# Two more expert blocks loaded ahead of the last load of the first mixer, and sums of squares made as columns

## The chip, the core and the metric

The kernel runs on one core of a Trainium2 chip. Its time is device microseconds (us) of one execution. Before the change three runs took 1422.38, 1422.58 and 1422.58 us; the median is 1422.58 us. One further execution was recorded by the hardware profiler; every row below comes from it.

## What is computed

Two transformer blocks on one sequence of 256 tokens with 1024 channels, all in float32. Only the parts that the change touches are shown.

```
# block 1
u = modulate(rmsnorm(h, g_norm1), sh1, sc1)
y = hybrid_mixer(u, ...)            # ends with:  merged = gate0*y_conv + gate1*y_gla ;  y = merged @ w_out
h = h + ga1 * y
u2 = modulate(rmsnorm(h, g_norm2), sh2, sc2)
h = h + ga2 * hierarchical_moe(u2)  # 4 groups x 8 experts, top 2 inside the best group
x = modulate(rmsnorm(h, g_final), shf, scf)
# block 2
x = x + mixer2(rmsnorm_2(x, ln1_g)) ;  x = x + conv_ffn(rmsnorm_2(x, ln2_g)) ;  return rmsnorm_2(x, final_g)

rmsnorm(x, g) = x * rsqrt(mean(x*x) + 1e-6) * g
# routing: lg = u2 @ w_rg + b_rg ;  le = u2 @ w_re + b_re   (4 + 32 columns)
# experts: hid = silu(t @ w1[e]) * (t @ w3[e]) ;  y += comb[:, e] * (hid @ w2[e])
#          w1, w3: 32 x 1024 x 512, w2: 32 x 512 x 1024 (float32), all of them are read
```

## The kernel before

**Layout.** Activations lie turned: 128 channels on the partitions, 8 tiles of them, 256 tokens along the row (`h`, `u`, `sq`). The whole memory of a partition is one tensor `arena` of 40870 columns, cut by hand, and a pair of regions that follow each other in time at its end (`fine1`, then `above`; then `fine2`). Most projections split each weight piece into a high part (ScalarE) and a rest (VectorE) and make three products for each pair; `advance(name, n)` on an engine does its share for n pieces, `flush` finishes what is begun. A piece is 8 x 256 columns (1 MiB). Pieces arrive in a ring of three slots of 2048 columns (`ring`, at the start of `arena`).

**The experts.** Their 192 MiB come as 96 blocks of 2 MiB (`WIDE` = 4096 columns), 12 for each of 8 quads of experts: four of w1, four of w3, four of w2. `wides` holds 8 places; block n goes to place n mod 8. Block n of 8 and more waits until TensorE is done with block n - 8 (`up_made`, `down_made`). The first three blocks have places that come free early (`early`) and are issued among the loads of the first mixer; place 3 is columns 0 to 4095, that is two slots of the ring, free when the last piece of `w_out` is split; places 4 to 6 are `above`, free when the last products of `w_out` are made (`products_of[PIECES1 - 1, 1]`); place 7 waits for a sum of the norm.

**The loads.** Every load of weights is issued by SyncE in one fixed order (`sync_program`); a load that waits holds back all loads behind it. `ada(j)` loads the two half chunks 2j and 2j + 1 of the modulation weights (1 MiB each); chunks 24 to 31 (`w_ada_f`) are loaded between the pieces `pw`, `gla_o` and `w_out` and summed by TensorE in `ada_sums(12)` to `ada_sums(15)`, each of which frees a slot for a later chunk.

**The norms.** `norm(i)` on TensorE multiplies a 128 x 128 matrix of ones with the squares (8 products of 256 columns), which gives the sum over channels on all partitions; ScalarE takes the root of 128 x 256, VectorE the reciprocal of 128 x 256 (`rstd`) and multiplies. Norm 0 opens block 1; norm 1 is ahead of the routing and is spelled out by itself; norms 2 and 3 stand between the experts and block 2; norm 4 is ahead of the convolutional FFN. `spin(n)` issues n products that nobody reads. After norm 1 the logits are made as 36 rows of 256 tokens, scaled by `rstd`, given a bias, and turned by TensorE to columns (tokens on the partitions); `rstd` itself is also turned.

## Time and profile before

| | us |
|---|---|
| median of three runs | 1422.58 |
| profiled execution, its time | 1423.39 |
| its span | 1421.6 |
| TensorE busy (matmuls) | 1207.6 (85%) |
| VectorE busy | 675.5 (48%) |
| ScalarE busy | 449.9 (32%) |
| the chain that ended last: TensorE, DMA, VectorE, SyncE's queue | 56%, 18%, 12%, 7% of the span |

In the rows, PE is TensorE's matmuls and PEld its weight loads, DVE is VectorE, ACT is ScalarE, SPq is SyncE's issuing of DMAs. A line such as L1293 or L2098 is that of a helper through which an engine's operations pass, so operations are told apart by shape and time. A float32 matmul stands in the trace as two records, a float32r one and a transpose as one. PEclk is the share of full clock granted to TensorE.

### The profile page before, as it was taken

Reading aid. Unit: us, or ns where it says so; the run is one execution under the profiler, and the core shown is the slowest. Engines: PE = TensorE matmul, PEld = TensorE weight load, DVE = VectorE, ACT = ScalarE, POOL = GpSimd, SP = SyncE. Lnnn points to the kernel's source line nnn. Section 1 sums busy time; section 2 is a strip of 40 time slices with the busy share of each in tenths; the row PEclk is TensorE's granted clock in tenths of the full one; section 3 lists DMA queues with packets and bytes.
Section 4 is the critical chain, followed back from the end, with each engine's and each line's share of the span. In section 5 each row is a group of like instructions: output and inputs, shape, how many; then the busy total and the mean of one; then the engine's idle time right before and its main releaser. Section 6 shows DMA issues by size and latency. Waiting matters only on the chain.

```text
span 1421.6 us, 20416 instructions
## 1 busy us (share of the span) xinstructions
PE 1207.6 (85%) x8784; PEld 955.0 (67%) x8784; DVE 675.5 (48%) x1146; ACT 449.9 (32%) x643; POOL 2.2 (0%) x16
## 2 busy tenths in 40 slices
PE   6999999999765657566575899999999999999998
PEld 3789897886322213222231599899998889999986
DVE  2657986554110101101010464465657786668974
ACT  2543343432000000000000353443545454555453
POOL 0000000000000000000000000000000000000000
PEclk9999999999988878788897999999999999999999
DMA  9887862978999999999999676343543425355552
GB/s 350 302 284 264 269 149 106 360 246 356 420 420 420 419 420 420 420 420 420 419 420 416 221 223 191 111 129 119 162 155 114 149 94 196 115 174 179 183 204 87
DMA packets 169555, 374.06 MB, mean 263 GB/s; under 512 B 8257, under 2 KB 121299, under 8 KB 145780
## 3 DMA queue, kind: packets, MB, share of 16 engines
q1 hardware_dynamic: 166940, 369.12, 70.4%
q0 software_dynamic: 144, 3.54, 0.8%
q8 instruction: 71, 1.16, 0.4%
q10 hardware_dynamic: 2376, 0.04, 0.1%
q14 instruction: 24, 0.20, 0.0%
HBM read 371.59 MB, written 4.62 MB: 265 GB/s over the span
## 4 chain that ended last, share of the span: by engine, by line
PE 56%; DMA 18%; DVE 12%; SPq 7%; ACT 4%; issue 2%; DVEq 0%; ACTq 0%
PE bank L617 30%; DMA arena<-in_w 13%; SPq L2638 7%; PE bank L1270 4%; DVE arena L1301 4%; PE bank L930 4%; DVE fine L1293 3%; ACT fine L2098 2%; DVE arena L1293 2%; DMA above<-in_w 2%; PE bank L971 2%; PE bank L614 2%; PE bank L897 2%; DVE arena L1298 1%; PE bank L648 1%
## 5 line engine op out<-in xcount | busy, mean ns | idle before, releaser
L617 PE MATMUL bank<-fine 128*128 128x256 f32 x4512 | 561.5, 286 | 17.4 <-DVE fine L1293 17.4
L617 PEld LDWEIGHTS bank<-fine 128*128 128x128 f32 x4512 | 550.6, 194 | 31.1 <-issue 21.6
L1293 DVE TENSOR_TENSOR fine<-arena,fine 128x1024 fp32r<-128x1024 f32 (+2 forms) x263 | 299.7, 1168 | 175.2 <-ACT fine L2098 165.8
L2098 ACT ACTIVATE fine<-arena 128x1024 fp32r<-128x1024 f32 (+2 forms) x279 | 266.5, 984 | 183.8 <-PE bank L617 84.6
L2098 ACT ACTIVATE arena<-bank 128x256 f32<-128x256 f32 (+2 forms) x153 | 68.0, 472 | 530.0 <-PE bank L942 187.4
L930 PE MATMUL bank<-arena 128*32 128x512 f32 x640 | 123.4, 795 | 56.8 <-DMA arena<-in_w 37.5
L1293 DVE TENSOR_TENSOR arena<-arena,bank 128x512 f32<-128x512 f32 x8 | 8.4, 1053 | 288.8 <-PE bank L930 288.8
L930 PE MATMUL bank<-above,arena 128*32 128x512 f32 x384 | 77.1, 734 | 56.8 <-issue 24.7
L2098 ACT ACTIVATE arena<-arena 128x512 f32<-128x512 f32 (+6 forms) x90 | 61.1, 708 | 152.0 <-DVE arena L1301 63.1
L1301 DVE SCALAR_TENSOR_TENSOR arena<-arena 128x256 f32<-128x256 f32 (+3 forms) x262 | 107.6, 484 | 1.1 <-ACT arena L2098 0.8
L930 PEld LDWEIGHTS bank<-arena 128*32 128x32 f32 x640 | 30.6, 140 | 112.8 <-issue 111.5
L930 PEld LDWEIGHTS bank<-above,arena 128*32 128x32 f32 x384 | 20.1, 131 | 111.2 <-issue 109.1
L1293 DVE TENSOR_TENSOR arena<-arena 128x512 f32<-128x512 f32 (+7 forms) x130 | 82.6, 661 | 9.3 <-ACT arena L2098 7.9
L1293 DVE TENSOR_TENSOR arena<-bank,arena 128x256 f32<-128x256 f32 (+8 forms) x92 | 36.8, 436 | 49.5 <-PE bank L1078 17.6
L1270 PE MATMUL bank<-fine 128*128 128x512 f32 x264 | 60.3, 390 | 0.0
L971 PE MATMUL bank<-arena 128*32 128x512 f32 x304 | 46.6, 667 | 14.3 <-DMA arena<-in_w 10.9
L1779 DVE COPY arena<-bank 128x512 f32<-128x512 f32 x8 | 5.5, 692 | 107.6 <-PE bank L971 92.3
L1270 PEld LDWEIGHTS bank<-fine 128*128 128x128 f32 x264 | 49.4, 188 | 10.7 <-DVE fine L1293 0.3
L614 PE MATMUL bank<-fine 128*128 128x256 f32 x384 | 47.6, 284 | 1.0 <-DVE fine L1293 1.0
L614 PEld LDWEIGHTS bank<-fine 128*128 128x128 f32 x384 | 46.5, 192 | 2.0 <-issue 2.0
L565 PE MATMUL bank<-arena 128*128 128x256 f32 x152 | 38.3, 393 | 0.8 <-ACT arena L2098 0.8
L1298 DVE TENSOR_SCALAR arena<-bank,arena 128x128 f32<-128x128 f32 x96 | 30.9, 385 | 16.9 <-PE bank L897 16.6
(177 smaller groups left out, 810.8 us busy)
## 6 DMA issues: line engine op xcount, KB each, us to landing
arena<-in_w SPq DMA_DIRECT2D x118, 1024.0 KB, 26.5
above<-in_w SPq DMA_DIRECT2D x66, 1024.0 KB, 26.5
arena<-in_w_in SPq DMA_DIRECT2D x62, 1024.0 KB, 5.5
arena<-in_w_ada SPq DMA_DIRECT2D x24, 1024.0 KB, 9.6
arena<-in_ffn_w_up SPq DMA_DIRECT2D x22, 1024.0 KB, 5.1
arena<-in_ffn_w_down SPq DMA_DIRECT2D x11, 1024.0 KB, 5.0
arena<-in_w_ada_f SPq DMA_DIRECT2D x8, 1024.0 KB, 9.4
above<-in_w SPq DMA_DIRECT2D x12, 512.0 KB, 17.9
```

Source lines behind the costliest of these rows:

```text
L565: e.matmul(bank[:, 0:256], ident, consts[:, 0:256], start=True, stop=True, skip_group_check=True)
L614: ins = e.matmul(o, x[:, kt, j * P:j * P + P], w[:, k, :], start=start, stop=stop, skip_group_check=True)
L617: ins = e.matmul(o, w[:, k, j * P:j * P + P], x[:, kt, :], start=start, stop=stop, skip_group_check=True)
L897: ins = e.matmul(bank[:, j * P:j * P + P], uT[:, tc, k * P:k * P + P], hot2[:, tc, quad * P:quad * P + P], start=tc == 0, stop=tc == 1)
L930: ins = e.matmul(bank[32 * x:32 * x + 32, :], xg[:, i, 4 * th + k, 32 * x:32 * x + 32], slots[x // 2][:, x % 2, k, :], start=th == 0 and k ...
L971: ins = e.matmul(ob[c][32 * x:32 * x + 32, :], hidT[:, i, 2 * th + k, 32 * x:32 * x + 32], slots[x // 2][:, x % 2, k, 512 * c:512 * c + 51 ...
L1270: ins = e.matmul(obs[tc][c][:, :], x, w[:, cs], start=n == i == 0, stop=n == 21 and i == 2, skip_group_check=True)
L1293: return e.tensor_tensor(o, a, b, f)
L1298: return e.tensor_scalar(o, a, s_1, s_2, f1, f2)
L1301: return e.scalar_tensor_tensor(out=o, in0=a, scalar=s, in1=b, op0=f1, op1=f2)
L2098: return e.activation(o, i, f, bias=bias, scale=scale)
L2638: e.dma_start(slot[:, x, :, :], src[quad, :, 2 * (i % 2) + x, at:at + kt, :]).then_inc(*wide_in[s].up(n, 16))
```

## The change

The places of the blocks and the loads: `early` gets a fourth place, where `q`, `kk` and `v` of the first mixer lay, and the fifth block goes to slots 1 and 2 of the ring, free once the last piece but one of `w_out` is split. The place that waited for a sum of the norm is gone. Of the two half chunks behind `ada(12)` the second comes behind the loads of `pw`; the first three blocks of `w_out` come ahead of the third expert block. The norms: the squares become the stationary operand and one column of ones the moving one, so that a norm's sum is two columns with tokens on the partitions; root and reciprocal are of 128 x 2, and `as_row` brings the result back as a 128 x 256 row tile in PSUM, from which VectorE multiplies. The routing keeps columns throughout. Three warm-up groups of six products: one stays, two become two.

```diff
-        ada_slots2 = [arena[:, q_at:q_at + SLOT], flat(v), arena[:, consts1_at:consts1_at + SLOT]]
+        ada_slots2 = [arena[:, xbase:xbase + SLOT], arena[:, consts1_at:consts1_at + SLOT], flat(u)]
...
-        early = [arena[:, at:at + WIDE] for at in (early_at + WIDE, early_at + 2 * WIDE, early_at)]
-        wides = early + [arena[:, 0:WIDE]] + [above[:, WIDE * i:WIDE * i + WIDE] for i in range(FINE // WIDE)] + [
-            arena[:, WIDE:2 * WIDE]]
+        early = [arena[:, at:at + WIDE] for at in (early_at + WIDE, early_at + 2 * WIDE, early_at, q_at)]
+        wides = early + [arena[:, SLOT:SLOT + WIDE]] + [above[:, WIDE * i:WIDE * i + WIDE] for i in range(FINE // WIDE)]
...
-                    ins = e.matmul(bank[:, 0:256], ones, squares[:, k, :], start=k == 0, stop=k == KT - 1)
+                    for tc in range(2):
+                        ins = e.matmul(bank[:, tc:tc + 1], squares[:, k, tc * P:tc * P + P], ones[:, 0:1], start=k == tc == 0,
+                                       stop=k == KT - 1, skip_group_check=True)
...
+            def as_row(o, tc):
+
+                return e.matmul(o, rstd_of[:, tc:tc + 1].to_broadcast([P, P]), ident, start=True, stop=True, skip_group_check=True)
...
-                    ins = e.matmul(raw[0:36, 0:256], wr[:, k, :], h[:, k, :], start=k == 0, stop=k == KT - 1)
+                    for tc in range(2):
+                        ins = e.matmul(raw[:, 36 * tc:36 * tc + 36], h[:, k, tc * P:tc * P + P], wr[:, k, :], start=k == tc == 0,
+                                       stop=k == KT - 1, skip_group_check=True)
...
             norm(2)
+            norm_row(2)
             spin(6)
             norm(3, u)
-            spin(6)
+            norm_row(3)
+            spin(2)
...
             norm(4)
-            spin(6)
+            norm_row(4)
+            spin(2)
...
-                e.reciprocal(rstd, rstd).then_inc(*normed.up((i, "r")))
-                e.wait_ge(*normed[i, "r"])
+                e.reciprocal(rstd_of, rstd_of).then_inc(*normed.up((i, "r")))
+                e.wait_ge(*rms_row[i])
                 for g in range(2):
-                    tt(sq[:, 4 * g:4 * g + 4, :], x[:, 4 * g:4 * g + 4, :], repeat(rstd, 4), ALU.mult).then_inc(*normed.up((i, g)))
+                    tt(sq[:, 4 * g:4 * g + 4, :], repeat(bank_of(normed, (i, 1))[:, 0:256], 4), x[:, 4 * g:4 * g + 4, :],
+                       ALU.mult).then_inc(*normed.up((i, g)))
...
+                    elif f == 25:
+                        e.wait_ge(*act_on["conv"])
                     elif f == 26:
-                        e.wait_ge(*act_on["conv"])
+                        e.wait_ge(*x_lo_v["og", 1])
...
-            ada(12)
+            ada(12, (0,))
             load("pw", 2)
+            ada(12, (1,))
...
-            load("gla_o", 1)
+            load("gla_o", 2)
+            ada(14)
+            load("w_out", 3)
+            ada(15)
+            load("w_out", 1)
             expert(0, 2)
-            load("gla_o", 1)
-            ada(14)
-            load("w_out", 2)
-            ada(15)
-            load("w_out", 2)
+            expert(0, 3)
```

**The loads on SyncE, from `pw` to the end of the first mixer.** `in_w` is an expert block (two DMAs each), `in_w_ada_f` a half chunk. Before:

```order
L2600 DMA arena<-in_w_gla_o 128x8x256 [waits conv_out]
L2638 DMA arena<-in_w 128x2048 [waits o_turned]
L2638 DMA arena<-in_w 128x2048
L2600 DMA arena<-in_w_gla_o 128x8x256 [waits w_lo_by_vector]
L2581 DMA arena<-in_w_ada_f 128x4x512 [waits ada_sum] x2
L2600 DMA arena<-in_w_out 128x8x256 [waits w_lo_by_vector] x2
L2581 DMA arena<-in_w_ada_f 128x4x512 [waits ada_sum] x2
L2600 DMA arena<-in_w_out 128x8x256 [waits w_lo_by_vector] x2
L2638 DMA arena<-in_w 128x2048 [waits w_lo_by_vector]
L2638 DMA arena<-in_w 128x2048
L2638 DMA above<-in_w 128x2048 [waits products]
```

The same place now:

```order
L2632 DMA arena<-in_w_gla_o 128x8x256 [waits conv_out]
L2632 DMA arena<-in_w_gla_o 128x8x256 [waits w_lo_by_vector]
L2613 DMA arena<-in_w_ada_f 128x4x512 [waits ada_sum] x2
L2632 DMA arena<-in_w_out 128x8x256 [waits w_lo_by_vector] x3
L2613 DMA arena<-in_w_ada_f 128x4x512 [waits ada_sum] x2
L2632 DMA arena<-in_w_out 128x8x256 [waits w_lo_by_vector]
L2670 DMA arena<-in_w 128x2048 [waits o_turned]
L2670 DMA arena<-in_w 128x2048
L2670 DMA arena<-in_w 128x2048 [waits o_turned]
L2670 DMA arena<-in_w 128x2048
L2670 DMA arena<-in_w 128x2048 [waits w_lo_by_vector]
```

The third block went behind `w_out`, the fourth joins it there, and the fifth waits for VectorE instead of standing behind the last split piece.

**TensorE from the raw logits to the ranks of the routing.** Before:

```order
L851 MATMUL bank<-arena 36x256 x4
L858 MATMUL bank<-arena 128x256
L860 MATMUL bank<-arena 128x256
L851 MATMUL bank<-arena 36x256 x4
L867 MATMUL bank<-arena 128x128 x8
L875 MATMUL bank<-arena 128x1 x2
L880 MATMUL bank<-arena 128x36 x2
L867 MATMUL bank<-arena 128x128 x8
L565 MATMUL bank<-arena 128x256 x4
L888 MATMUL bank<-arena 128x64
```

Now (L873 are the raw logits, L879 the squares, L896 the turning of `h`):

```order
L873 MATMUL bank<-arena 128x36 x8
L879 MATMUL bank<-arena 128x1 x4
L873 MATMUL bank<-arena 128x36 x8
L896 MATMUL bank<-arena 128x128 x16
L567 MATMUL bank<-arena 128x256 x4
L907 MATMUL bank<-arena 128x64
```

The two turnings (L875, L880) between the halves of the turning of `h` are gone, and the sums have twice the products.

## Rows read from the trace of the kernel before

**Rows 1.** The page: GB/s of DMA in 40 slices of 35.5 us.
```profile
GB/s 350 302 284 264 269 149 106 360 246 356 420 420 420 419 420 420 420 420 420 419 420 416 221 223 191 111 129 119 162 155 114 149 94 196 115 174 179 183 204 87
```
**Rows 2.** Stretches: length, busy time per engine (count), PEclk, DMA share, GB/s.
```profile
309.00:321.00 12.00, 12.00 (x103) 12.00 (x102) 6.12 (x9) 4.70 (x6) 0.00 (x0) 1.00 0.01 2
...
329.00:330.00 1.00, 1.00 (x6) 0.52 (x5) 0.96 (x4) 0.49 (x1) 0.00 (x0) 1.00 0.71 106
330.00:331.00 1.00, 1.00 (x5) 0.58 (x4) 0.67 (x2) 0.98 (x2) 0.00 (x0) 1.00 0.78 221
331.00:332.00 1.00, 1.00 (x6) 0.44 (x5) 0.00 (x0) 0.92 (x2) 0.00 (x0) 1.00 0.92 385
```
**Rows 3.** Timeline of SyncE's queue: start, length, line, DMAs issued.
```profile
328.59 3.21 SPq L2638 DMA_DIRECT2D above<-in_w  x6
...
346.63 8.64 SPq L2638 DMA_DIRECT2D arena<-in_w  x8
```
**Rows 4.** Timeline of TensorE, 268 to 331 us: start, length, [idle before, releaser].
```profile
275.24 1.07 PE L648 MATMUL bank<-arena 128*32 128x512 f32 x8 [0.42 <-DMA arena<-in_w_ada_f]
276.24 20.42 PE L617 MATMUL bank<-fine 128*128 128x256 f32 x168
296.58 1.92 PE L648 MATMUL bank<-arena 128*32 128x512 f32 x16
301.80 4.56 PE L617 MATMUL bank<-fine 128*128 128x256 f32 x24 [3.29 <-DVE fine L1293]
...
308.14 20.42 PE L617 MATMUL bank<-fine 128*128 128x256 f32 x168
```
**Rows 5.** A stretch inside the 4.56 us of rows 4.
```profile
303.00:304.50 1.50, 1.50 (x9) 1.50 (x9) 0.40 (x1) 1.48 (x2) 0.00 (x0) 0.50 1.10 356
```
**Rows 6.** Source line L2600 (loads of pieces), 236 to 330 us.
```profile
DMA to landing us min/median/max: 5.2/11.0/15.4
```
**Rows 7.** Timeline of ScalarE, 236 to 330 us.
```profile
247.99 3.97 ACT L2098 ACTIVATE arena<-arena 128x256 f32<-128x256 f32 x6 [1.78 <-DVE arena L1293]
...
295.73 2.95 ACT L2098 ACTIVATE fine<-arena 128x1024 fp32r<-128x1024 f32 x3 [6.43 <-DMA arena<-in_w_out]
```
**Rows 8.** Timeline of all engines, 319 to 354 us (routing, first expert products).
```profile
331.40 1.92 PE L851 MATMUL bank<-arena 128*36 128x256 f32 x8
...
334.19 0.51 PE L875 MATMUL bank<-arena 128*128 128x1 f32 x4
...
335.49 0.17 DVE L1689 TENSOR_REDUCE arena<-bank 128x2 f32<-128x8 f32 x1 [0.79 <-PE bank L880]
...
336.75 1.89 PE L565 MATMUL bank<-arena 128*128 128x256 f32 x8
...
338.79 0.43 PE L888 MATMUL bank<-arena 128*128 128x64 f32 x2
...
342.94 3.65 PE L930 MATMUL bank<-arena 128*32 128x512 f32 x32 [0.30 <-DVE arena L1298]
```
**Rows 9.** Timeline of all engines, 764 to 826 us (norms 2 and 3).
```profile
806.70 2.00 ACT L2098 ACTIVATE fine<-arena 128x1024 fp32r<-128x1024 f32 x2 [2.21 <-DMA arena<-in_w_in]
...
813.86 0.47 ACT L2098 ACTIVATE arena<-bank,arena 128x256 f32<-128x256 f32 x1 [1.22 <-PE bank L669]
...
816.23 2.36 DVE L1293 TENSOR_TENSOR arena<-arena 128x1024 f32<-128x1024 f32 x2
```
**Rows 10.** Groups by form, whole program: total busy, mean ns, idle before.
```profile
L1740 DVE RECIPROCAL arena<-arena 128x2 f32<-128x2 f32 x1 | 0.2, 167 | 0.0
...
L1293 DVE TENSOR_TENSOR arena<-bank,arena 128x512 f32<-128x512 f32 x16 | 10.7, 689 | 21.8 <-PE bank L1078 7.3 <-PE bank L1270 6.6 <-PE bank L1165 5.5
...
L1293 DVE TENSOR_TENSOR arena<-arena,bank 128x512 f32<-128x512 f32 x8 | 8.4, 1053 | 288.8 <-PE bank L930 288.8
```
**Rows 11.** Timeline of all engines, 1196 to 1236 us (norm 4).
```profile
1215.19 3.62 PE L669 MATMUL bank<-arena 128*128 128x256 f32 x16
```
**Rows 12.** Timeline of all engines, 0 to 62 us.
```profile
18.57 1.06 PE L648 MATMUL bank<-arena 128*32 128x512 f32 x8 [1.54 <-DMA arena<-in_w_ada]
```

More of the change, by code:

```diff
@@ L682, in tensor_program @@
             ada_sums(0)
+            norm_row(0)
             ada_sums(1)
@@ L831, in tensor_program @@
                 ins.then_inc(*conv_out.up(m0))
+            bank = misc(route, "bias row")
+            e.wait_ge(*route["bias"])
+            e.matmul(bank[:, 0:36], col("router_b")[0:36, :].to_broadcast([36, P]), ident[0:36, 0:36], start=True, stop=True).then_inc(
+                *router.up("bias row"))
             spin(3)
@@ L850, in raw_logits, with sum_squares @@
                 for k in (2 * pair, 2 * pair + 1):
-                    ins = e.matmul(raw[0:36, 0:256], wr[:, k, :], h[:, k, :], start=k == 0, stop=k == KT - 1)
+                    for tc in range(2):
+                        ins = e.matmul(raw[:, 36 * tc:36 * tc + 36], h[:, k, tc * P:tc * P + P], wr[:, k, :], start=k == tc == 0,
+                                       stop=k == KT - 1, skip_group_check=True)
+                return ins
+            def sum_squares(k, start):
+                for tc in range(2):
+                    ins = e.matmul(bank[:, tc:tc + 1], sq[:, k, tc * P:tc * P + P], ones[:, 0:1], start=start and tc == 0,
+                                   stop=not start, skip_group_check=True)
                 return ins
@@ L857, in tensor_program @@
             e.wait_ge(*squares["most"])
-            e.matmul(bank[:, 0:256], ones, sq[:, 0, :], start=True, stop=False)
+            sum_squares(0, True)
             e.wait_ge(*squares["last"])
-            e.matmul(bank[:, 0:256], ones, sq[:, 6, :], start=False, stop=True).then_inc(*norm_sum.up(1))
+            sum_squares(6, False).then_inc(*norm_sum.up(1))
             raw_logits(2)
@@ L871, in tensor_program @@
             turn_h(0, 1)
-            bank = misc(route_a, "rstd")
-            e.wait_ge(*normed[1, "r"])
-            for tc in range(2):
-                ins = e.matmul(bank[:, tc:tc + 1], rstd[:, tc * P:tc * P + P], ident[:, 0:1], start=True, stop=True)
-            ins.then_inc(*router.up("rstd"))
-            bank = misc(route, "logits")
-            e.wait_ge(*route["columns"])
-            for tc in range(2):
-                ins = e.matmul(bank[:, 36 * tc:36 * tc + 36], lgc[0:36, tc * P:tc * P + P], ident[0:36, 0:36], start=True, stop=True)
-            ins.then_inc(*router.up("logits"))
             turn_h(1, 0)
@@ L992, in tensor_program @@
             with e.If_ne(reg, 0):
+                for tc in range(2):
+                    ins = as_row(banks[0][:, 256 + tc * P:256 + tc * P + P], tc)
+                ins.then_inc(*general_t.up("row"))
+                e.wait_ge(*general_v["u", 1])
                 e.wait_ge(*route["combO"])
@@ L1682, in vector_program @@
             e.wait_ge(*normed[1, "r"])
-            step(tt(lgc[0:36, :], bank_of(route, "columns")[0:36, 0:256], rstd[0:36, :], ALU.mult))
-            ts(lgc[0:36, :], lgc[0:36, :], col("router_b")[0:36, :], ALU.add).then_inc(*route.up("columns"))
-            e.wait_ge(*router["logits"])
-            logits = shaped(bank_of(route, "logits")[:, 0:72], 2, 36)
+            e.wait_ge(*route["bias row"])
+            raw = bank_of(route, "columns")
+            logits = shaped(lgc[:, 0:72], 2, 36)
+            stt(logits[:, 0, :], raw[:, 0:36], rstd_of[:, 0:1], bias_row, ALU.mult, ALU.add).then_inc(*route.up())
+            step(stt(logits[:, 1, :], raw[:, 36:72], rstd_of[:, 1:2], bias_row, ALU.mult, ALU.add), "columns")
             l4, le = logits[:, :, 0:4], logits[:, :, 4:36]
@@ L1782, in vector_program @@
                 e.wait_ge(*sent[7])
+                e.wait_ge(*general_t["row"])
                 for g in range(2):
-                    tt(u[:, 4 * g:4 * g + 4, :], h[:, 4 * g:4 * g + 4, :], repeat(rstd, 4), ALU.mult).then_inc(*general_v.up(("u", g)))
+                    tt(u[:, 4 * g:4 * g + 4, :], repeat(banks[0][:, 256:512], 4), h[:, 4 * g:4 * g + 4, :], ALU.mult).then_inc(
+                        *general_v.up(("u", g)))
                 for k in range(KT):
@@ L2570, in sync_program, with ada @@
         def sync_program(e):
-            def ada(j):
-                for f in (2 * j, 2 * j + 1):
+            def ada(j, halves=(0, 1)):
+                for f in (2 * j + i for i in halves):
                     s, mem, prior = ada_slot(f)
```

40 lines of the change are left out of this document (23 added, 17 removed).

## The prediction

> **What bounds the kernel now.** I read the DMA line of the page first, because the experts are 192 MiB. From slice 11 to slice 22 it stands at 419 to 420 GB/s without a dip [rows 1]: from about 330 to 790 us the kernel is a DMA stream, and nothing inside it that TensorE, VectorE or ScalarE do costs time. A block of 2 MiB (2.10 MB) takes 2.10 / 0.42 = 5.0 us there. So what this stage is worth is decided at its front: how many blocks are in when the stream starts, and when it starts. The second view is the windows just ahead of it. Between 309 and 321 us the DMA moves 2 GB/s: it is idle for 12 us while TensorE works full time at full clock on the last pieces of `w_out` [rows 2, 4]. SyncE issues the three `above` blocks at 328.59 us, right behind the last product of `w_out` at 308.14 + 20.42 = 328.56 [rows 3, 4]. Call that moment p. The third view, TensorE's timeline, says what sets p: two breaks, one behind a half chunk at 275.24 and one of 3.29 us ahead of the first product of `w_out`; this piece landed only at 295.7, where ScalarE had waited 6.43 us for it [rows 4, 7]. From 796 us on TensorE bounds the rest, with the norms 3 and 4 on the path.
>
> **The front of the stream, before.** After a dry queue the stream does not run at once: from 328.59 to 332 it should have moved 1.43 MB and moved 0.71 (0.11 + 0.22 + 0.39 in the three rows), which is 1.7 us lost [rows 2, 3]. Places 4 to 7 follow each other without a gap, so the queue is drained at p + 1.7 + 4 x 5.0 = p + 21.7. Block 8 needs the first expert products: they end at 342.94 + 3.65 = 346.6, that is p + 18.0, and SyncE issues at 346.63 [rows 3, 8]. It had 3.7 us in hand; from there 88 blocks run at the DMA's rate.
>
> **The front after.** At p five blocks are in, or issued, instead of three and one. Blocks 2 and 3 stand behind the last piece of `w_out`: issued by about 301, landed about 317. Block 4 waits for the piece but one of `w_out`, about 310, so it is queued before the queue is dry and is in at about 322. All three fill the 12 idle microseconds. At p only three blocks are left that wait for nothing but p: drained at p + 1.7 + 15.0 = p + 16.7. But block 8 still waits for the first expert products, and now these are late. That is the new wait, and behind it on SyncE stands the whole rest of the stream. So of the 5.0 us that the extra block could bring, the stage gets only what the products allow: with r for what the routing saves, they end at p + 18.05 - r, and the stream restarts 1.7 later.
>
> The routing, r. Before, the first reduce of the logits starts at 335.49 = p + 6.93 [rows 8]. After, the path is raw logits and squares on TensorE, then two VectorE operations of about 0.2. A weight load with a product of one column takes 0.51 / 4 = 0.128 us per record [rows 8]; the first half of the logits has 16 records (2.0), the squares 8 (1.0), the second half 16 (2.0): p + 5.0, then 0.3 for the two operations: p + 5.3. Before, these products took the same 1.92 per half with half the records [rows 8]. The two turnings and their handovers go, VectorE's mask is 1.6 us earlier. TensorE itself then comes later than the mask: from p + 5.0 it has 16 turnings (2.1) and four warm-up products (1.89), so the ranks start at p + 9.0, where they were at 338.79 = p + 10.2 [rows 8]. r = 1.2; its bounds are 0 (if the warm-ups and banks hold it) and 1.6. The small root (about 0.2, as other ScalarE operations on two columns) and the reciprocal of 128 x 2 at 0.167 for 1.75 [rows 10] hide behind the second half of the logits.
>
> **How much earlier p comes, x.** The queue serves loads in order. Ahead of the first `w_out` piece stand 2 MiB fewer, 5.0 us: landed at about 290.7 in place of 295.7 [rows 7]. Against it: chunk 25 now waits for the activation of the convolution, the fourth of six operations that start at 247.99 and take 3.97, so about 250 [rows 7]; a load into an idle queue lands after 5.2 us [rows 6], the later ones 2.5 to 2.9 apart (1.05 MB at the 420 GB/s of the stream or the 356 GB/s of the tenth slice [rows 1]). Counting on from 250 through `gla_o` 0, block 0, `gla_o` 1, block 1 and chunk 26, chunk 27 lands at 276.1 to 276.3, 1.0 later than now; the products of `gla_o` then run from 277.2 to 297.6 (20.4), the sums of `ada(14)` to 299.5. The first half of `w_out` needs its split, which VectorE has ready by about 297; so it runs at once and at full clock, 2.9 us, to 302.4. Now there are 3.29 us of break and 4.56 us in place of 2.9. In that stretch the granted clock is 0.50, that is 1.2 GHz, after those 3.29 idle us [rows 4, 5]. Chunk 31 can be issued only behind the first sum of `ada(14)`, 298.7, and lands 5.2 later at 303.9; its sum ends at 304.9, and the last seven halves (20.4) at 325.3. x = 328.6 - 325.3 = 3.3. Bounds: 0.5, if the loads run at 2.9 throughout and chunk 27 comes 3.5 late, and 4.9, if chunk 31 does not hold.
>
> **Sum for the stream.** Gain = (p + 21.7) - (p - x + 18.05 - r + 1.7) = 1.95 + x + r = 1.95 + 3.3 + 1.2 = 6.4 us. Bounds 2.5 and 8.5. The Trainium skill (DMA: Bandwidth & Descriptors, Specifications) gives a first-byte latency of about 0.6 us for loads issued by SyncE; the three rows show 1.7 us lost at such a start. By the page the restart would cost 1.1 less and the gain would be 7.5, an estimate; I stay with the rows.
>
> **Norms.** Norm 0: TensorE's next sums wait 1.54 us for a modulation chunk at 18.57 anyway [rows 12]; the new row product (0.6) lies in that. Nothing. Norm 2: ScalarE splits the first piece of `q2` before it squares for norm 3, and that piece lands at 806.7; it goes on at 808.7, while the new norm 2 is done at about 806.8 [rows 9]. Nothing either, its saving is hidden by the load. Norm 3: from the end of its products to the first multiplication there are 813.86 to 816.23, 2.4 us. After: root 0.2, reciprocal 0.2, the row product 0.6 with two handovers 0.2: 1.2. The products get 0.1 longer, since the last pair is paced by ScalarE (8 records at 0.128 for 0.92). Gain 1.1. Norm 4: here TensorE has all pairs but one at its start: 3.62 before [rows 11], 32 x 0.128 = 4.1 after; gain 1.2 - 0.45 = 0.8. The multiplication from PSUM: no row of 128 x 1024 exists; with the bank as first operand 128 x 512 takes 689 ns, like from `arena`, with the bank second and strided 1053 [rows 10]. I take the first, as the code has the bank first; by the other each norm loses 0.7 to 1.4, down to nothing or a small loss. The Trainium skill (TensorE: Matmul & The Clock Gate, LDWEIGHTS) says a weight load costs by its columns, P/1.2 ns, which speaks against squares as weights: 107 ns for 128. By that the 32 records of norm 4 would be 3.4 us, an estimate, and norm 4 would gain 1.4; my row has 0.128 per record with its product.
>
> Sum: 6.4 + 1.1 + 0.8 = 8.3 us. The profiled execution took 1423.39 (span 1421.6), so it would take 1415.1; the median is 0.8 lower, 1422.58 - 8.3 = 1414.3.
>
> **Rivals.**
> *A, the new order does not move p* (x = 0.5: chunk 27 or 31 holds TensorE). For it: the loads from 237 to 307 us are limited by the DMA, and the new order adds two dry spots (248 to 250, and ahead of chunk 31). Against it: 2 MiB less ahead of `w_out`. Gain 1.95 + 0.5 + 1.2 + 1.9 = 5.5: 1417.0. Chance 0.2.
> *B, the stream does not run dry* because the routing saves more than 3 us or the tail of three blocks lasts longer. Then the gain is 5.0 + x, 8.3, and the total 10.2: 1412.4. For it: the two ends, p + 16.7 and p + 16.85, are close; against it: to hide the restart the products must come 1.7 sooner yet. Chance 0.15.
> *C, the half chunk blocks the line.* Chunk 25 and chunk 26 now wait for ScalarE's activation and for VectorE's rest of `og`, and on SyncE all of `gla_o`, the blocks and `w_out` stand behind them; `og` in turn is split behind `gla_o` 0, which is loaded behind chunk 25. Each microsecond past the reserve falls 1:1 on p, and TensorE falls to half clock in the break. It decides when p comes over 1.95 + 1.2 = 3.2 us later than now, with the norms over 5.1, that is when `gla_o` ends 8.4 us later than I count. If chunk 27 landed 12 us later than counted, at 288, p would be 8.7 later than now and the kernel at 1426. Against it: my count has the queue full until 273. Chance 0.05.
> *D, the routing is no shorter and the multiplication from PSUM is slow*: r = 0, norms together 0. Gain 1.95 + 3.3 = 5.2: 1417.3. Chance 0.1. With fewer warm-up products (six to two) the granted clock may fall at norms 3 and 4; the rows give 1.6 us for 24 products at half clock, twice that for both.
>
> **Chances.** Forecast 0.5, A 0.2, B 0.15, D 0.1, C 0.05. The range that leaves out 2 in 10 reaches from B to a little past A and D: 1411.0 to 1419.0. About 0.2%, 2.8 us, is what a measurement of this kernel tells from no change. Faster by more than that: all of the forecast and B, nearly all of A and D: 0.88. Within: 0.07. Slower: 0.05, from C.
>
> **What the profile after would show.** The stretch from 309 to 321 at about 400 GB/s instead of 2. No break ahead of the first half of `w_out`, that row at 2.9 and not 4.56; the last half ending near 325.3; a short break for chunk 31. SyncE issuing `above` at p and block 8 about 16.9 later, with a hole of 1 to 2 us in the GB/s there: that hole is the point of the forecast; without it B holds. The ranks at p + 9.0. The first fall of the GB/s line below 400, now at about 790 us, 6.4 earlier. Norm 3 and norm 4 with 1.2 between last product and first multiplication, and the multiplication at 1.22. I am wrong if p is not earlier, if the stream has a second hole further on, or if PEclk is below 1.00 behind norms 3 and 4.

## The result, and the profile after

| | before | after |
|---|---|---|
| median, us | 1422.58 (12 runs, 1421.27 to 1423.82) | 1425.9 (12 runs, 1420.08 to 1430.01) |
| ratio | | 1.0025, 95% interval 1.0016 to 1.0034 |
| profiled execution, its time | 1423.39 | 1428.46 |
| its span | 1421.6 | 1426.6 |
| mean granted clock of TensorE | 0.946 | 0.935 |

The changed kernel is a little slower: by 3.3 us, where a gain of 8.3 was forecast. The direction of the forecast is wrong, and the time lies outside its range. The runs after also spread over 10 us where those before spread over 2.6, so times are compared by their medians.

**The front of the stream.** First the page's row of the GB/s, in 40 slices (it answers to [rows 1]).

```profile
GB/s 347 296 284 257 276 153 89 346 333 302 419 420 419 419 420 418 419 420 419 420 420 415 207 214 192 118 120 119 155 158 116 148 94 195 112 173 180 183 203 89
```

The plateau begins in slice 11 and ends in slice 22 as before; slice 10 is 302 in place of 356. The windows at the front answer to [rows 2]: length, busy time by engine, PEclk, DMA share, GB/s.

```profile
308.00:312.00 4.00, 3.40 (x29) 2.17 (x26) 1.78 (x2) 0.54 (x1) 0.00 (x0) 1.00 1.10 381
...
344.00:348.00 4.00, 3.70 (x38) 2.25 (x40) 1.37 (x4) 0.00 (x0) 0.00 (x0) 1.00 0.78 320
348.00:352.00 4.00, 3.50 (x36) 2.19 (x31) 0.60 (x2) 0.00 (x0) 0.00 (x0) 1.00 0.38 98
```

The 12 idle microseconds are filled, as forecast: 381 GB/s here and 418 to 424 from 312 to 324, instead of 2. The forecast hole is there too, at 344 to 352, and it is larger: 320 and 98 GB/s. Against 420 that is 1.7 MB too few, about 4 us, where 1 to 2 were forecast (an estimate from these two windows). SyncE's queue says why (answers to [rows 3]).

```profile
330.43 3.20 SPq L2670 DMA_DIRECT2D above<-in_w  x6
...
349.43 2.00 SPq L2670 DMA_DIRECT2D arena<-in_w  x4
```

`above` is issued at 330.43, not 3.3 us earlier but 1.8 later than before; block 8 is issued 19.0 behind it, where 16.9 was forecast and 18.0 stood before. So both x (how much earlier p comes) and r (what the routing saves) came out with the wrong sign. TensorE's timeline ahead of p (answers to [rows 4]):

```profile
276.77 1.06 PE L650 MATMUL bank<-arena 128*32 128x512 f32 x8 [1.21 <-DMA arena<-in_w_ada_f]
279.50 1.94 PE L650 MATMUL bank<-arena 128*32 128x512 f32 x8 [1.67 <-DMA arena<-in_w_ada_f]
281.37 21.11 PE L619 MATMUL bank<-fine 128*128 128x256 f32 x168
...
304.26 3.13 PE L619 MATMUL bank<-fine 128*128 128x256 f32 x24
...
309.99 20.41 PE L619 MATMUL bank<-fine 128*128 128x256 f32 x168
```

The break of 3.29 us and the slow 4.56 us of [rows 4] are gone: the first half of `w_out` stands at 304.26 with 3.13 and no idle time before it. But the products of `gla_o` begin at 281.37, 5.1 us later than at 276.24, behind two waits for half chunks (1.21 and 1.67 us where there was one of 0.42). The sum at 279.50 took 1.94 us for 8 products, the one above it 1.06.

The routing, with the clock (answers to [rows 8]):

```profile
332.15 1.05 PE L879 MATMUL bank<-arena 128*128 128x1 f32 x8
333.07 2.64 PE L873 MATMUL bank<-arena 128*128 128x36 f32 x16
335.51 3.65 PE L896 MATMUL bank<-arena 128*128 128x128 f32 x16
338.96 2.89 PE L567 MATMUL bank<-arena 128*128 128x256 f32 x8
341.69 0.33 PE L907 MATMUL bank<-arena 128*128 128x64 f32 x2
...
345.73 3.65 PE L949 MATMUL bank<-arena 128*32 128x512 f32 x32 [0.30 <-DVE arena L1324]
```

The second number is the time of the group. The logits of 16 records take 1.87 us in the first half, ahead of these rows, and 2.64 in the second; 16 turnings take 3.65, the eight warm-up products 2.89 where [rows 8] have 1.89. The count's product starts at 341.69 = p + 11.3 (before p + 10.2, forecast p + 9.0). The windows of the changed kernel show the clock:

```profile
334.00:336.00 2.00, 2.00 (x13) 2.00 (x13) 0.20 (x2) 0.00 (x0) 0.00 (x0) 0.54 1.01 422
338.00:340.00 2.00, 2.00 (x9) 1.82 (x8) 1.36 (x12) 1.65 (x4) 0.00 (x0) 0.50 1.01 426
```

The same of the kernel before:

```profile
334.00:336.00 2.00, 1.62 (x15) 1.45 (x14) 1.11 (x6) 1.24 (x3) 0.00 (x0) 1.00 1.04 438
338.00:340.00 2.00, 1.28 (x7) 0.74 (x6) 1.17 (x6) 1.97 (x7) 0.00 (x0) 1.00 1.04 438
```

The third number from the end is PEclk: 0.54 and 0.50 in place of 1.00. TensorE runs at 1.2 GHz instead of 2.4, and the engine is busy for 2.00 of 2.00 us.

**The norms.** TensorE around norm 3 before (L669 the sums of squares, L565 the warm-ups, L575 the first ffn products):

```profile
809.83 4.00 PE L669 MATMUL bank<-arena 128*128 128x256 f32 x16 [3.26 <-ACT arena L2098]
813.66 2.75 PE L565 MATMUL bank<-arena 128*128 128x256 f32 x12
818.14 5.98 PE L575 MATMUL bank<-fine 128*128 128x256 f32 x48 [1.73 <-ACT fine L2098]
```

After (L672 the sums of squares, L678 the row product, L567 the warm-ups, L577 the first ffn products):

```profile
805.88 1.20 PE L678 MATMUL bank<-arena 128*128 128x128 f32 x4 [0.71 <-DVE arena L1460]
806.87 5.30 PE L567 MATMUL bank<-arena 128*128 128x256 f32 x12
811.99 3.72 PE L672 MATMUL bank<-arena 128*128 128x1 f32 x32
817.41 1.91 PE L567 MATMUL bank<-arena 128*128 128x256 f32 x4
819.56 7.17 PE L577 MATMUL bank<-fine 128*128 128x256 f32 x48 [0.24 <-ACT fine L2130]
```

And its windows there:

```profile
806.00:808.00 2.00, 2.00 (x7) 1.82 (x8) 0.89 (x1) 1.12 (x2) 0.00 (x0) 0.50 1.10 348
...
816.00:818.00 2.00, 1.58 (x6) 1.51 (x7) 0.51 (x2) 0.01 (x1) 0.00 (x0) 0.50 1.02 331
```

Twelve warm-up products take 5.30 us in place of 2.75, a row product 1.20 (0.6 was forecast), 48 ffn products 7.17 in place of 5.98. Before, PEclk is 1.00 in both windows. The multiplication from PSUM is as forecast, 1.22:

```profile
817.65 1.22 DVE L1319 TENSOR_TENSOR arena<-bank,arena 128x1024 f32<-128x1024 f32 x1 [1.38 <-PE bank L678]
```

**The ledger.** Four places hold the 5.0 us by which the span of the profiled execution grew (the medians differ by 3.3). TensorE before, and after:

```profile
796.27 3.69 PE L985 MATMUL bank<-arena 128*128 128x256 f32 x16 [0.81 <-ACT arena L2098]
...
907.28 3.11 PE L617 MATMUL bank<-fine 128*128 128x256 f32 x24 [1.33 <-DVE fine L1293]
```

```profile
797.47 3.69 PE L1004 MATMUL bank<-arena 128*128 128x256 f32 x16 [0.81 <-ACT arena L2130]
...
909.89 4.58 PE L619 MATMUL bank<-fine 128*128 128x256 f32 x24 [1.33 <-DVE fine L1319]
...
1219.35 4.75 PE L672 MATMUL bank<-arena 128*128 128x1 f32 x32
```

The end of the stream (the first product behind the experts, 796.27 and 797.47) is 1.2 later. From there to the first products behind norm 3's (823.96 and 826.57) another 1.4 is lost. At 909.89 a group of 24 products takes 4.58 instead of 3.11, a loss of 1.5. From norm 4's first sum (1215.19 and 1219.35) to 1228.95 and 1233.99 it is 0.9 more. That makes 5.0.

The 1.5 us at 909.89 are not the change's. The same group, behind the same 1.33 idle us, is slow in e8 too, which has the norms and warm-ups of before:

```profile
903.31 4.59 PE L618 MATMUL bank<-fine 128*128 128x256 f32 x24 [1.33 <-DVE fine L1294]
```

In the fourteen traces of this case it takes 3.11 nine times and 4.58 to 4.61 five times (after, e7, e8, e10, e12). A second group of the same kind loses 1.5 us in the kernel before itself:

```profile
1166.25 27.64 PE L617 MATMUL bank<-fine 128*128 128x256 f32 x216 [1.91 <-DVE fine L1293]
```

It takes 27.6 in before, after, e1 and e8 and 26.15 in the other ten. The clock is at 0.62 and 0.53 in the two windows behind its start, and at 1.00 there in e6. So a single profiled execution can be 1.5 or 3 us longer for reasons that have nothing to do with the edit.

### The profile page after: what moved, and what is told of

It reads as the page before. It is cut to its first block, busy times and chain, and to the rows that moved or that the text cites. A ratio compares the mean times of both kernels' runs of the same rounds, so it can differ in the third digit from the quotient of the medians.

```text
span 1426.6 us, 20576 instructions
## 1 busy us (share of the span) xinstructions
PE 1221.3 (86%) x8862; PEld 971.5 (68%) x8862; DVE 668.0 (47%) x1147; ACT 449.6 (32%) x642; POOL 2.2 (0%) x16
## 3 DMA queue, kind: packets, MB, share of 16 engines
q8 instruction: 72, 1.18, 0.4%
## 4 chain that ended last, share of the span: by engine, by line
PE 57%; DMA 14%; DVE 12%; SPq 11%; ACT 3%; issue 3%; ACTq 0%; DVEq 0%
PE bank L619 30%; SPq L2670 8%; DMA above<-in_w 7%; DMA arena<-in_w 6%; DVE arena L1327 5%; PE bank L1296 4%; PE bank L949 3%; DVE fine L1319 3%; PE bank L990 2%; SPq L2666 2%; ACT fine L2130 2%; DVE arena L1319 2%; PE bank L616 2%; DVE arena L1324 1%; PE bank L650 1%
## 5 line engine op out<-in xcount | busy, mean ns | idle before, releaser
L949 PE MATMUL bank<-arena 128*32 128x512 f32 x640 | 113.7, 755 | 74.7 <-DMA arena<-in_w 37.8
L949 PEld LDWEIGHTS bank<-arena 128*32 128x32 f32 x640 | 30.4, 134 | 152.3 <-issue 148.9
L1319 DVE TENSOR_TENSOR arena<-arena 128x512 f32<-128x512 f32 (+8 forms) x125 | 73.5, 612 | 9.3 <-ACT arena L2130 7.9
L1319 DVE TENSOR_TENSOR arena<-bank,arena 128x256 f32<-128x256 f32 (+7 forms) x96 | 45.4, 509 | 60.3 <-PE bank L1103 18.2
L990 PE MATMUL bank<-arena 128*32 128x512 f32 x304 | 44.5, 662 | 17.2 <-DMA arena<-in_w 11.3
L1296 PEld LDWEIGHTS bank<-fine 128*128 128x128 f32 x264 | 49.4, 188 | 10.7 <-DVE fine L1319 0.3
L990 PEld LDWEIGHTS bank<-arena 128*32 128x32 f32 x304 | 12.8, 120 | 43.7 <-issue 43.7
L567 PE MATMUL bank<-arena 128*128 128x256 f32 x136 | 39.6, 435 | 0.8 <-ACT arena L2130 0.8
```

The lines of the kernel that those rows point to most:

```text
L567: e.matmul(bank[:, 0:256], ident, consts[:, 0:256], start=True, stop=True, skip_group_check=True)
L949: ins = e.matmul(bank[32 * x:32 * x + 32, :], xg[:, i, 4 * th + k, 32 * x:32 * x + 32], slots[x // 2][:, x % 2, k, :], start=th == 0 and k ...
L990: ins = e.matmul(ob[c][32 * x:32 * x + 32, :], hidT[:, i, 2 * th + k, 32 * x:32 * x + 32], slots[x // 2][:, x % 2, k, 512 * c:512 * c + 51 ...
L1296: ins = e.matmul(obs[tc][c][:, :], x, w[:, cs], start=n == i == 0, stop=n == 21 and i == 2, skip_group_check=True)
L1319: return e.tensor_tensor(o, a, b, f)
```

## The experiments

Theory N: the narrow products (one column moving, in long runs) let TensorE's clock fall, and that is the loss. Theory L: the new order of the loads is. Theory G: the fewer warm-up products are. Ratios are against runs of the kernel before on the same chip, with 95% intervals. The sets e1 to e4, e5 to e8 and e9 to e12 ran on three chips; the kernel before has medians of 1423.08, 1422.53 and 1422.74 there, and a gain or loss is counted against the one of its set. Stretches and rows are from each one's profiled execution.

| | what | median, us | ratio |
|---|---|---|---|
| e1 | loads alone | 1419.82 | 0.9980 (0.9971 to 0.9988) |
| e2 | norms alone, one column | 1425.49 | 1.0023 (1.0014 to 1.0032) |
| e3 | the change, 128 columns | 1417.9 | 0.9957 (0.9943 to 0.9972) |
| e4 | before, narrow warm-ups | 1427.53 | 1.0040 (1.0027 to 1.0053) |
| e5 | e3, chunks as before | 1414.78 | 0.9942 (0.9927 to 0.9957) |
| e6 | norms alone, 128 columns | 1420.13 | 0.9982 (0.9971 to 0.9993) |
| e7 | the change, 32 columns | 1422.89 | 1.0002 (0.9989 to 1.0016) |
| e8 | e1, chunks as before | 1420.39 | 0.9977 (0.9967 to 0.9988) |
| e9 | e5 with more warm-ups | 1415.56 | 0.9956 (0.9943 to 0.9969) |
| e10 | the change again | 1425.42 | 1.0016 (1.0003 to 1.0029) |
| e11 | e5 again | 1413.16 | 0.9933 (0.9920 to 0.9945) |
| e12 | e3, one column in the routing | 1418.19 | 0.9969 (0.9957 to 0.9981) |

**e1, e2: the two halves of the change.** e1 takes the places, the waits and the order of the loads and leaves the norms; e2 takes the norms and the routing and leaves the loads. Of the change's diff, in e1:

```diff
+        early = [arena[:, at:at + WIDE] for at in (early_at + WIDE, early_at + 2 * WIDE, early_at, q_at)]
```

and in e2:

```diff
+                        ins = e.matmul(bank[:, tc:tc + 1], squares[:, k, tc * P:tc * P + P], ones[:, 0:1], start=k == tc == 0,
```

> Only the places of the blocks and the order of the loads are changed; norms and routing are those of before. Theory N (the norms' and the routing's narrow products let TensorE's clock fall to 1.2 GHz, and that costs what the change loses): PEclk stays 1.00 in the routing and behind norms 3 and 4; the first expert products end 18.0 behind the last product of w_out as before, the last product is about 0.6 later than before (rows of the changed kernel less its 1.2 us shift from the start), the stream restarts at once behind a dry queue: gain 1.95 - 0.6 = 1.3, median near 1421.3, and the runs lie as close together as those of before (within 3 us). Theory L (the order of the loads is the loss): as slow as the changed kernel, 1425 or more.

> Only norms and routing are changed; places and loads are those of before. Theory N: PEclk 0.50 in the second half of the routing's logits and behind the sums of norms 2, 3 and 4; the routing is 1.0 later, all of it in the stream only as far as the queue's reserve of 3.7 us is used up (so nothing), norms 2 to 4 cost 1.1 + 2.6 as in the changed kernel: median 1426 to 1428, spread over 5 us or more. Theory L: 1420.7, that is 1.9 better than before (norm 3 1.1, norm 4 0.8), since the loads are the old ones.

The loads alone gain 3.3 us, the norms alone lose 2.4; theory L falls. In e1 the end of the stream is at 793.01, 3.3 earlier than at 796.27, and p at 327.1, 1.5 earlier. Theory N had expected p 0.6 later and a gain of 1.3; the loads did better than that.

**e3: the same products, wider.** The squares stay the weights, but 128 equal columns of ones stream through, and the root reads one column of each 128. A record takes nearly the same time either way: 32 of them 3.70 to 3.72 us in the rows of norms 2 and 3 after, 3.81 to 4.02 in e3.

```diff
-                        ins = e.matmul(bank[:, tc:tc + 1], squares[:, k, tc * P:tc * P + P], ones[:, 0:1], start=k == tc == 0,
+                        ins = e.matmul(bank[:, tc * P:tc * P + P], squares[:, k, tc * P:tc * P + P], ones, start=k == tc == 0,
...
```

> The changed kernel with the sums of squares made by 128 columns of ones instead of one column: same count of products and weight loads, same waits, same two warm-up products, the result stands in 128 equal columns of which one is read. The 32 logit records of 36 columns in the routing are left. Theory N: PEclk 1.00 behind norms 2, 3 and 4, the twelve records of warm-ups behind norm 2 take 2.75 and not 5.1, the first piece behind norms 3 and 4 takes 6.0 and not 7.2: 4 to 6 us better than the changed kernel, 1420 to 1422. Theory G (the clock falls because TensorE stands still for 0.7 us ahead of the row product and has fewer warm-ups behind it): the standstills are the same, so the same 0.50 and 1425 to 1427.

It stands 5.2 us under before where the change stands 3.3 above, about 8 us between them and more than the 4 to 6 that theory N expected. TensorE around norm 3 in e3:

```profile
805.72 0.68 PE L678 MATMUL bank<-arena 128*128 128x128 f32 x4 [0.71 <-DVE arena L1460]
806.24 2.76 PE L567 MATMUL bank<-arena 128*128 128x256 f32 x12
809.02 4.02 PE L672 MATMUL bank<-arena 128*128 128x128 f32 x32
...
816.50 5.98 PE L577 MATMUL bank<-fine 128*128 128x256 f32 x48 [1.08 <-ACT fine L2130]
```

The 32 records of sums take 4.02 (one column: 3.72), and what stands around them is fast: 0.68, 2.76 and 5.98 instead of 1.20, 5.30 and 7.17. The number of warm-ups is that of the change, so theory G has nothing to explain. From the first sum of norm 3 to the first ffn product it takes 7.48 us (809.02 to 816.50) against 8.31 before (809.83 to 818.14): 0.8 gained, 1.1 was forecast.

**e4: narrow products without the rest of the change.** In the kernel before the three groups of warm-ups become products of one column.

```diff
+            def narrow(n):
...
+                for _ in range(2 * n):
+                    e.matmul(banks[b][:, 0:1], ident, consts[:, 0:1], start=True, stop=True, skip_group_check=True)
...
-            spin(6)
+            narrow(6)
```

> Kernel of before; only the warm-up products behind norms 2, 3 and 4 (6 each, 256 columns, 12 records in 2.75 us) are replaced by 12 products each of one column (24 records, about 2.8 us). No wait and no result depends on them; TensorE is occupied for as long. Theory N: PEclk falls to 0.50 behind them, the products behind (norm 3's sums, the first pieces of q2 and up) take 1.2 to 2 us longer each: 1425 to 1428. Theory G: TensorE does not stand still longer than before, PEclk stays 1.00 and the time 1422.6.

TensorE of e4 from the end of norm 2 to the ffn:

```profile
803.11 2.73 PE L572 MATMUL bank<-arena 128*128 128x1 f32 x24
808.54 6.20 PE L676 MATMUL bank<-arena 128*128 128x256 f32 x16 [2.70 <-ACT arena L2105]
819.05 8.10 PE L582 MATMUL bank<-fine 128*128 128x256 f32 x48 [1.60 <-ACT fine L2105]
```

The same 16 records of sums as before take 6.20 instead of 4.00, the same 48 ffn products 8.10 instead of 5.98. In the kernel before the idle time ahead of these sums was even longer, 3.26 us against 2.70, and the clock held. So the pause alone does not do it; what differs is what the engine did before it. The loss is 4.5 us (1427.53 for 1423.08).

**e5, e8: why p did not come earlier.** The half chunks go back to their old places and waits (both ahead of `pw`, chunk 26 behind the convolution's activation); the fourth block then waits for the sum of chunk 31. e5 does this in e3, e8 in e1.

```diff
-        ada_slots2 = [arena[:, xbase:xbase + SLOT], arena[:, consts1_at:consts1_at + SLOT], flat(u)]
+        ada_slots2 = [arena[:, q_at:q_at + SLOT], flat(v), arena[:, consts1_at:consts1_at + SLOT]]
...
-                    elif f == 25:
-                        e.wait_ge(*act_on["conv"])
                     elif f == 26:
-                        e.wait_ge(*x_lo_v["og", 1])
+                        e.wait_ge(*act_on["conv"])
...
+                    elif n == 3:
+                        e.wait_ge(*ada_sum[31])
```

> The changed kernel with the 128-column ones (as in the run before), and with w_ada_f's chunks back in the places and with the waits that they had before: chunk 26 asks for the convolution's SiLU, not for og's second half, both chunks of the step go ahead of pw, and the fourth block of the experts, which lies on two of these places, waits for the sum of chunk 31. Theory M (the move of the chunks' places is what kept p from coming earlier: the sum of chunk 27 stood 1.41 and 1.69 us in TensorE's row at 274.65 and 277.40 of the run with the loads alone, where before lost 0.42 us at 275.24): gla_o's products start at about 276.2 after the same start, p about 2 us earlier than in the run with 128-column ones (329.5), the whole about 2 us less than its 1417.9: 1415.9. Rival H (the chunks come late because more bytes stand ahead of them in the queue, whatever place they go to): the same waits of over 1 us at the sums of chunks 26 and 27 are there, the time stays at 1417.9. Rival W (the fourth block's wait for chunk 31 holds SP and leaves a second hole before 330): a slice of the DMA row under 200 GB/s between 304 and 320, and a time above 1418.

> The kernel before with the change of the loads alone, and w_ada_f's chunks in the places and with the waits that they had before, the fourth block waiting for the sum of chunk 31. Theory M: 2 us under the run with the loads alone (1419.8), 1417.8, with gla_o's products starting at 276 instead of 278.40 and p at about 325. Rival H: no difference, 1419.8.

TensorE of e1, then of e8, at the two half chunks:

```profile
274.65 1.07 PE L649 MATMUL bank<-arena 128*32 128x512 f32 x8 [1.41 <-DMA arena<-in_w_ada_f]
277.40 1.06 PE L649 MATMUL bank<-arena 128*32 128x512 f32 x8 [1.69 <-DMA arena<-in_w_ada_f]
```

```profile
274.69 1.06 PE L649 MATMUL bank<-arena 128*32 128x512 f32 x8
277.48 1.07 PE L649 MATMUL bank<-arena 128*32 128x512 f32 x8 [1.73 <-DMA arena<-in_w_ada_f]
```

The wait for chunk 26 goes (1.41 to nothing), the one for chunk 27 stays (1.73). The executions start from different places: the products of `pw` begin at 251.78 in e1 and at 253.29 in e8. From there to the first product of `gla_o` it is 26.6 and 25.2 us; for e3 and e5, from 252.86 and 251.85, it is 27.6 and 25.6, of which 0.8 is a sum at a lower clock in e3 (1.83 for 1.07). In both pairs the stretch is 1.4 to 2.0 shorter, which is the size that theory M forecast. But p itself is only 0.25 earlier in e8 than in e1 (326.83 for 327.08), and half of rival H's sign is there: the wait for chunk 27 is over 1 us in e5 and e8 (in e11, the kernel of e5 again, neither wait is there). The time of e8 is the one that H forecast: it gains 2.1 us on before, e1 3.3, with intervals that lie on each other. Against e3's 5.2, e5 gains 7.8 and e11 9.6; the interval of e5 overlaps that of e3, and the one of e11 meets its edge. So the old places of the chunks are probably worth 2 to 4 us with wide norms, and are not shown to be worth anything with the old norms. Rival W is not seen: e5 moves 393 to 422 GB/s from 304 to 320.

**e6: the norms alone, wide.** e2 with the edit of e3.

> The kernel before with the columns for the norms and the routing, but with 128 equal columns of ones in place of one; no change of the loads. Theory N (the narrow products' clock was the loss): the clock stays at 1.00 over norms 2, 3 and 4 and the forecast sizes of the norms show: norm 3 and norm 4 0.8 to 1.1 us each less from the first sum to the first ffn product (8.31 and 7.93 us before), the routing 1.0 to 1.6 us less from p to the turns of the counts (10.2 before); the whole 2 to 3.5 us under before, 1420.0. If instead it is only the loads that earn and the rest is neutral at best, it stays within 1 us of before.

5.4 us less than e2, 2.4 less than before (1422.53 in that set). From first sum to first ffn product norm 3 takes 7.37 us (8.31 before) and norm 4 7.07 (7.93 before): 0.9 each. The count's product is at p + 8.5 (p + 10.2 before), which earns nothing here, since block 8 has its 3.7 us in hand as before. These are about the sizes that the forecast gave. Since e2 and e6 differ by nothing but the width, this pair shows the cost of the single column without any change of the loads.

**e7: 32 columns.** The change with `ones[:, 0:32]` as the moving operand.

```diff
+                        ins = e.matmul(bank[:, 32 * tc:32 * tc + 32], squares[:, k, tc * P:tc * P + P], ones[:, 0:32], start=k == tc == 0,
...
```

> The changed kernel with 32 equal columns of ones moving in place of one (the run with 128 gave 1417.9, the one with one column 1425.9). The products are bound by their weight load in all three widths, so a record should be as long at full clock (3.7 us for 32). Theory N as a matter of the columns that stream through the array: 32 are too few, the clock falls to 0.50 behind the sums as with one, and the time stays within 1.5 us of 1425.9. Rival: any width above one does, and the time is that of 128 columns, 1418.

TensorE around norm 3:

```profile
804.70 3.92 PE L567 MATMUL bank<-arena 128*128 128x256 f32 x12
...
815.69 6.70 PE L577 MATMUL bank<-fine 128*128 128x256 f32 x48 [0.49 <-ACT fine L2130]
```

Between the two: 3.92 for the twelve warm-ups (2.76 at 128 columns, 5.30 at one), 6.70 for the ffn products. The routing ran at full speed there. 1422.89 is neither of the two forecasts: less is lost than with one column, and the clock still falls behind the norms.

**e9: more warm-ups on the good base.** e5 with twelve products behind norms 3 and 4.

```diff
-            spin(2)
+            spin(6)
```

> The changed kernel with 128 columns of ones and the chunks of w_ada_f as before (1414.8 in the last set), with twelve warm-up products behind norms 3 and 4 in place of four. Theory N: the clock there is at 1.00 with four already, so more of them earn nothing; they take 2.75 us in place of 1.03 and end about 0.6 us ahead of the first ffn product at the earliest, so they hide: 1414.8, within 1.5 us. Rival G (the fewer warm-ups cost clock at the first ffn products): a gain of 1 us or more, 1413.5.

No gain: 1415.56 against 1413.16 for e11, which ran on the same chip. From norm 3's row product to the first ffn product it is 2.9 us against 2.6, so the eight products more do not quite hide. Theory G falls a second time.

**e10, e11: once more.** The changed kernel and e5, each without an edit, on a third chip.

> The changed kernel itself once more, on the same chip as the three others of this set. Both theories: 2 to 4 us slower than before, and 8 to 11 us slower than with 128 columns and the old chunks; if the chip drew it slow by chance the first time, it stands at or under before here.

> The version with 128 columns of ones and the chunks as before once more (1414.78, ratio 0.9942 in the last set), for its interval: ratio between 0.993 and 0.996 to before. Rival: the last set drew it fast, and it stands at the 0.9957 of the version with the new chunk places.

The change stands at 1.0016, again slower; e11 at 0.9933, 9.6 us under before and 12.3 under the change. It is the best version. In its profiled execution, TensorE and SyncE's queue at the front:

```profile
274.70 1.92 PE L650 MATMUL bank<-arena 128*32 128x512 f32 x16
276.56 20.41 PE L619 MATMUL bank<-fine 128*128 128x256 f32 x168
...
333.45 0.43 PE L907 MATMUL bank<-arena 128*128 128x64 f32 x2 [0.34 <-DVE arena L1319]
```

```profile
325.01 3.24 SPq L2670 DMA_DIRECT2D above<-in_w  x6
...
341.30 7.94 SPq L2670 DMA_DIRECT2D arena<-in_w  x8
```

Here p is 325.0, close to the 325.3 of the forecast, the count's product starts 8.5 behind, and block 8 is issued 16.3 behind. In e5 p is 325.8. Of the 10.7 us between the profiled executions of before and e11, 6.2 are gained by the end of the stream (790.04 for 796.27), 2.1 over norms 2 and 3, 0.9 at norm 4, and 1.5 is the group of 216 products that ran slow in before only.

**e12: one column in the routing only.** Norms 0, 2, 3 and 4 keep 128.

```diff
-                    ins = e.matmul(bank[:, tc * P:tc * P + P], sq[:, k, tc * P:tc * P + P], ones, start=start and tc == 0,
+                    ins = e.matmul(bank[:, tc:tc + 1], sq[:, k, tc * P:tc * P + P], ones[:, 0:1], start=start and tc == 0,
```

> The changed kernel with 128 columns of ones in norms 0, 2, 3 and 4, and one column in the routing's norm alone (8 products). It splits the 8 us that one column costs. If the routing's clock carries its part (theory N with the routing: p + 8.6 to the counts' product with 128 columns, p + 11.3 with one, and block 8 waits for it one to one), it is 2 to 3 us slower than with 128 columns everywhere (1417.9): 1420.5, and the granted clock falls to 0.50 there. If eight narrow products between the logits of 36 columns are too few to matter, it stays at 1417.9 and the whole 8 us sit in the norms, the longer runs of 32.

TensorE in e12: the sums, the second half of the logits, the turnings.

```profile
330.33 1.24 PE L879 MATMUL bank<-arena 128*128 128x1 f32 x8
331.44 3.61 PE L873 MATMUL bank<-arena 128*128 128x36 f32 x16
334.86 3.41 PE L896 MATMUL bank<-arena 128*128 128x128 f32 x16
```

The profiled execution shows the fall in full: the second half of the logits takes 3.61 us instead of 1.87, the turnings 3.41 instead of 1.95, the clock is at 0.50 from 332 to 336, and the count comes at p + 11.3. The same eight products with one column were also traced in the changed kernel twice (the turnings take 3.65 both times) and in e2 (2.90), so the fall is there in all four traces; with 32 or 128 columns it is in none. What it costs the whole is less clear. e12 is 0.6 us behind e3 by the gains of their sets and 1.7 by the ratios, whose intervals overlap, where 2 to 3 were forecast. Against the change on its own chip it is 7.2 us faster (1425.42 and 1418.19). So most of the loss sits in the norms; the traces bound the routing's part at 2.8 us (p + 11.3 against p + 8.5 in e3), and how much of it reaches the time stays open. The profiled execution took 1422.47 us, the slowest of the six; 1.5 of that is the slow group of 24 products of the ledger (4.60).

## Why the prediction was wrong

**The step that failed is a sentence it did not have: what TensorE's clock does behind the new products.** Every price of the norms and the routing was a time at full clock. The clock stood only in rival D, for another reason (fewer warm-ups), with 0.1, and "slower" had 0.05, all of it for rival C. In e3 and e6, where the clock holds, those prices are right: norm 3 gains 0.8 to 0.9 (1.1 forecast), norm 4 0.9 (0.8), r is 1.7 (1.2). With one column norm 4 loses 0.9, r is -0.9 by the end of the first expert products (p + 19.0 for p + 18.05), and the stretch of norms 2 and 3 loses 1.4. "I am wrong if ... PEclk is below 1.00 behind norms 3 and 4" is what happened.

The trace had a warning: the only clock loss that I priced, [rows 5], I put down to 3.29 idle microseconds, while 3.26 idle microseconds ahead of norm 3's sums cost none. So idle time alone does not set the clock. The Trainium skill (TensorE: Matmul & The Clock Gate, "What's actually happening" in Part 1) says the gate follows how busy the engine has been. The profile's busy time alone does not tell that here: in the routing of the changed kernel TensorE is busy for 7.95 of the 8.00 us from 328 to 336, and the clock goes from 1.00 to 0.54.

**x = 3.3.** The half from the first product of `gla_o` to p was nearly right: it takes 49.0 us in place of 52.3, and 48.1 was forecast (277.2 to 325.3). That is 3.3 gained where the forecast had 4.2 there, less 1.0 lost ahead of it. The half ahead of `gla_o` was not right. It said that chunk 27 lands at 276.2, 1.0 later than before; it landed at 279.50. Of the 5.1 us by which p (330.40 by TensorE's rows) missed 325.3, 1.2 stood already at the start of the `pw` products (253.56 for 252.35; it lies between 250.28 and 254.80 in the fourteen traces, so this part is not shown to be the change's); 2.1 is the chunk, late behind the queue or behind chunk 26's new wait, which of the two is not shown; 0.9 is its sum at a lower clock; 0.7 the first products of `gla_o` (21.11 for 20.42); 0.2 lies in the rest. This is rival A's mechanism, with x = -0.6 once the start is taken out, below its 0.5. With the chunks as before, and norms of 128 columns, p comes where forecast (e11, e5).

**The sum for the stream.** The formula 1.95 + x + r came out near for two kernels: for e1 1.95 + 1.5 + 0.0 = 3.45 against 3.26 measured at the end of the stream, for the change 1.95 - 1.85 - 0.95 = -0.85 against -1.2. For three others it gave too much: in e11 1.95 + 3.6 + 1.8 = 7.3 stands against 6.2, in e5 1.95 + 2.8 + 1.8 = 6.5 against 4.8 (791.47 for 796.27), in e3 2.7 against -0.4. Part of this is found at the end of the stream. The last 32 products that wait for a block start 5.4 us earlier in e5 (767.78 for 773.14) and 1.8 earlier in e3 (771.38). They then take 6.29 and 6.51 us instead of 5.71, and in e3 six warm-ups behind them 2.90 instead of 1.53, so TensorE's clock gives back 0.6 and 2.2 there. The other 1 us or so in e3, e5 and e11 is not explained.

The restart's 1.7 us stands in both terms of that sum, in p + 21.7 and in the 1.7 behind the products, and cancels. So a shorter restart would have left the gain at 6.4, and the 7.5 of the prediction is a slip.

**Hidden costs.** Norm 0 and norm 2 were costed at nothing because loads cover them; e6 is 2.4 us faster as a whole, of which norms 3 and 4 explain 1.8, so nothing speaks against it. The multiplication from PSUM, the open price, took 1.22 as chosen. Rival C (the queue blocked for 8 us) did not happen.

## What to carry to other kernels

Price an operation on TensorE not only by its own time but by what the clock is after it. Here 32 records with a new stationary operand each took 3.7 us with one moving column and 3.8 to 4.0 with 128, and the single column left the work behind at half clock. Where one column is wanted, try equal columns that fill the time: it cost 0.1 to 0.3 us in a run of 32 records here and gave 8 us back. When an order of loads is changed, follow the small loads too: two half chunks of 1 MiB held TensorE for 1.21 and 1.67 us where one had held it for 0.42. And do not explain 1.5 us by two profiled executions: look whether the same group is slow in a kernel without the edit.

## What the runs showed of the hardware

Eight records of one column, between two groups of sixteen with 36 columns, were followed by a clock of 0.50 in all four traces that have them (after, e2, e10, e12); with 128 columns in those eight (e3) or 32 (e7) it stayed at 1.00. A fall can come without narrow products too: in e9's profiled execution the 128-column sums of norm 3, behind 2.11 idle us, took 5.46 instead of 4.02, and the two groups of the ledger, behind 1.33 and 1.91 idle us, lost 1.5 us each in five and in four of the fourteen traces. The times of the changed kernel spread more than those of the others with as many runs: 10.6 us over 12 runs in e10, against 6.9 over 12 in e6, and 7.2 over 29 runs of the kernel before on e6's chip. Reading PSUM as the first operand of a 128 x 1024 multiplication costs VectorE next to nothing against `arena`: 1.22 us against 2.36 / 2 = 1.18 in [rows 9].
